# A transformer kernel's first mixers: weighted sums written already turned, and the order of work around the last gate products

## The reference, cut to what matters

```python
gates = sigmoid(gate_logits)                    # 3 per nsa head
# nsa: 8 heads, three branches on the same queries
o_c = softmax(q @ k_compressed) @ v_compressed  # 15 compressed keys
o_s = softmax(q @ k_slc) @ v_slc                # 8 passes, "slc"
o_w = softmax(q @ k_win) @ v_win                # 8 passes, "win"
y_a = g0 * o_c + g1 * o_s + g2 * o_w
# moba: 8 heads of their own keys, causal       # 8 passes, "moba"
y_b = softmax(q @ k) @ v
gate_a, gate_b = split(sigmoid(h @ w_gbr))
merged = gate_a * (y_a @ w_up_nsa) + gate_b * (y_b @ w_up_moba)
x = x + g_m * (merged @ w_out)
```

## Time and profile before

| | |
|---|---|
| median of 3 runs | 2048.45 us |
| the profiled execution's own time | 2048.88 us |
| its span (first to last instruction) | 2047.0 us |
| PE busy | 1998.6 us, 98% |
| DVE busy | 1465.8 us, 72% |
| ACT busy | 1093.2 us, 53% |
| DMA, mean | 182 GB/s |

### The profile page before, as it was taken

How to read it: one execution, slowest core, us unless ns; L and a number is a source line. 1 busy time by engine, 2 the same in 40 slices (tenths; PEclk the granted TensorE clock), 3 DMA queues, 4 the chain that set the end, 5 groups by cost and what they waited for, 6 DMA issues and landing times. The chain is left out here.

```text
span 2047.0 us, 32169 instructions
## 1 busy us (share of the span) xinstructions
PE 1998.6 (98%) x12934; PEld 1775.0 (87%) x12934; DVE 1465.8 (72%) x2326; ACT 1093.2 (53%) x1732; POOL 23.6 (1%) x46
## 2 busy tenths in 40 slices
PE   7999999999999999999999999999999999999999
PEld 4889898898788988898888779888898899899888
DVE  7887778867786686567766676677667757767774
ACT  3555545535656455545545656655455536855552
POOL 1001000000010000000000000000000000000000
PEclk9999999999999999999999999999999999999999
DMA  9455458856455466555556324355555554235554
GB/s 353 157 205 196 167 181 275 273 207 187 145 201 211 147 224 206 185 186 185 186 190 201 125 102 144 130 187 187 186 177 187 186 181 137 93 124 163 187 175 134
DMA packets 266212, 372.23 MB, mean 182 GB/s; under 512 B 8400, under 2 KB 160336, under 8 KB 266064
## 3 DMA queue, kind: packets, MB, share of 16 engines
q1 hardware_dynamic: 264736, 368.91, 54.2%
q10 hardware_dynamic: 1328, 1.26, 0.2%
HBM read 369.09 MB, written 1.05 MB: 181 GB/s over the span
## 5 line engine op out<-in xcount | busy, mean ns | idle before, releaser
L2302 DVE TENSOR_TENSOR parts<-ring,parts 128x2048 fp32r<-128x2048 f32 (+2 forms) x304 | 675.8, 2223 | 396.1 <-ACT parts L721 395.4
L721 ACT ACTIVATE parts<-ring 128x2048 fp32r<-128x2048 f32 (+2 forms) x304 | 565.5, 1860 | 560.9 <-PE psum L1513 317.0
L1513 PE MATMUL psum<-h,parts 128*128 128x512 f32 x1920 | 675.9, 397 | 0.0
L1511 PE MATMUL psum<-h,parts 128*128 128x256 f32 x1920 | 539.0, 281 | 0.7 <-DVE parts L2302 0.5
L1513 PEld LDWEIGHTS psum<-h,parts 128*128 128x128 f32 x1920 | 360.6, 188 | 87.0
L1511 PEld LDWEIGHTS psum<-h,parts 128*128 128x128 f32 x1920 | 362.3, 189 | 2.5 <-DVE parts L2302 2.3
L1505 PE MATMUL psum<-h,parts 128*128 128x256 f32 (+1 forms) x2088 | 265.0, 285 | 4.5 <-DVE h L2311 2.0
L1505 PEld LDWEIGHTS psum<-h,parts 128*128 128x128 f32 (+1 forms) x2088 | 253.9, 190 | 7.3 <-issue 5.0
L1505 PE MATMUL psum<-parts,h 128*128 128x512 f32 (+1 forms) x864 | 204.9, 388 | 5.2 <-DVE h L2311 2.9
L1505 PE MATMUL psum<-hid_hl,parts 128*128 128x256 f32 x1584 | 189.4, 281 | 0.8 <-DVE parts L2302 0.6
L1505 PEld LDWEIGHTS psum<-hid_hl,parts 128*128 128x128 f32 x1584 | 188.0, 188 | 2.4 <-DVE parts L2302 2.4
(11 more groups left out here) (265 smaller groups left out, 2116.7 us busy)
## 6 DMA issues: line engine op xcount, KB each, us to landing
ring<-in_w_ffn_in SPq DMA_DIRECT2D x88, 512.0 KB, 4.8
ring<-in_ffn_w_gate SPq DMA_DIRECT2D x88, 512.0 KB, 3.7
ring<-in_ffn_w_up SPq DMA_DIRECT2D x88, 512.0 KB, 4.7
ring<-in_w_ada SPq DMA_DIRECT2D x43, 1024.0 KB, 5.4
ring<-in_w_in SPq DMA_DIRECT2D x36, 1024.0 KB, 5.0
ring<-in_ffn_w_down SPq DMA_DIRECT2D x32, 1024.0 KB, 4.9
ring<-in_w_ffn_out SPq DMA_DIRECT2D x16, 1024.0 KB, 5.1
ring<-in_ffn_w_down SPq DMA_DIRECT2D x16, 768.0 KB, 4.5
```

The costliest lines, as they stand in the source:

```text
L721: act.activation(out, in_, func, **kw).then_inc(*sig(name, *keys))
L1511: pe.matmul(bank[:, 0:S], wt_hl[1], act[:, 0, :], start=start, stop=False, skip_group_check=True)
L1513: return pe.matmul(bank.rearrange("p (a s) -> p a s", a=2), wt_hl[0], act, start=False, stop=stop, skip_group_check=True)
L2302: dve.tensor_tensor(out, a, b, op).then_inc(*sig(name, *keys))
```

## The change

Values become stationary: a pair of heads (n and n+1) writes its weighted sums by feature into partitions 0 to 63 and 64 to 127 of one bank (`turned_place`), with 256 moving columns for the first 128 keys and 128 for the second. slc, win and the compressed branch add up in banks 4 and 5, moba in 6 and 7. As the sums come out by feature, gate over sum must be applied earlier, by token: DVE makes `factor` for each head, and ACT multiplies the probabilities by it (`scaled`) ahead of the turning. The turning is three rounds behind the scores (`LATER`), and the loop has 28 rounds. The probabilities have four buffers and the turned ones three, instead of three and two. The transposes of `y`, `branch`, `moba_out` and the copy of the compressed output go; the compressed product is done at round 11, as four products of 256 columns. Gate products 6 and 7 are copied out ahead of any sigmoid. On DVE the splits at the last step of `gbr` go, so that the splits beyond w_up_nsa 0 come behind the products with the gates.

```diff
-HEADS, LAG, UNITS = 24, 2, 2
+HEADS, LAG, LATER, UNITS = 24, 2, 3, 2
...
+        def turned_place(bank, n):
+            half, c = HD * (n % 2), S * (n // 2 % 2)
+            return psum[half:half + HD, bank + n // 4, c:c + S]
...
@@ ACT
+            def scaled(head, n):
+                st, i = head["st"], head["i"]
+                buf = shifted_of(st, n)
+                act.wait_ge(*at(("factor", st, i)))
+                for t, (a, b) in enumerate(spans(head["mask"])):
+                    run(buf[:, a:b], buf[:, a:b], ACT.Copy, "act_scaled", ("scaled", st, i, t),
+                        scale=factor[:, n % 4, t:t + 1])
...
                             if n == 1 and k == 3 and i == 3:
-                                act.wait_ge(*at(("copied", ("gbr", l, 5))))
-                                run(br_gates[:, 1, 0:4], br_gates[:, 1, 0:4], ACT.Sigmoid,
-                                    "act_step")
                                 for q in (6, 7):
-                                    ...
-                                run(br_gates[:, 0], br_gates[:, 0], ACT.Sigmoid, "act_gates",
-                                    ("gates", l, 0))
+                                    copies(("gbr", l, q), br_e[:, 2 * q:2 * q + 2, :])
+                                act.wait_ge(*at(("copied", ("gbr", l, 7))))
+                                for a in range(2):
+                                    run(br_gates[:, a], br_gates[:, a], ACT.Sigmoid, "act_gates",
+                                        ("gates", l, a))
                                 act.preload_act_table_set(EXP_LN)
...
-                    if LAG <= i < HEADS + LAG:
-                        m = i - LAG
+                    if LATER <= i < HEADS + LATER:
+                        m = i - LATER
                         turned_copy(heads[m], base + m)
...
+                    if 1 <= i <= HEADS:
+                        scaled(heads[i - 1], base + i - 1)
...
@@ PE
+                def weighted_pair(i, first, done):
+                    pair = heads[i:i + 2]
+                    pe.wait_ge(*at(("copied", ("turn", pair[1]["st"], pair[1]["i"]))))
+                    probs = [prob_of(head["st"], base + i + n) for n, head in enumerate(pair)]
+                    for t, (a, c, q0) in enumerate(((0, S, 0), (S, S + P, P))):
+                        for n, head in enumerate(pair):
+                            ...
+                            mm = pe.matmul(head["o"][:, q0:S], head["v"][t], moving,
+                                           start=first and t == 0, stop=t == 1,
+                                           skip_group_check=True)
...
-            def moba_turn(l, j):
-                ...
-                for i in range(HEADS + LAG + 1):
+                for i in range(HEADS + LATER + 1):
                     if i < HEADS:
                         scores(i)
-                    if LAG <= i < HEADS + LAG:
-                        turn(i - LAG)
+                    if LATER <= i < HEADS + LATER:
+                        turn(i - LATER)
                     if i == 23:
                         next(more, None)
-                    if i > LAG:
-                        weighted(i - LAG - 1)
+                    if i > LATER and (i - LATER - 1) % 2:
+                        weighted_two(i - LATER - 2)
...
-                    if i == 6:
-                        ... (two products of 512 columns)
+                    if i == 11:
+                        compressed_out()
...
-                    if i == 21: ... tr y
-                    if i == 24:
-                        moba_turn(l, 0)
...
@@ DVE
-                                if k == 3:
+                                if k == 3 and (i, n) != (3, 1):
                                     splits.until((("gbr", l), i, n), 2)
...
-                def moba_out(p, pv): ...
-                def branch(b, kind): ...
+                def scaled(i):
+                    ...
+                    dve.wait_ge(*at(("probs", st_, head["i"], 1)))
+                    total, out = sums[:, column, :], factor[:, (base + i) % 4, :]
+                    ...
+                    if st_[0] == "moba":
+                        dve.reciprocal(out, total).then_inc(*sig("dve_step", done))
+                    else:
+                        dve.reciprocal(out, total).then_inc(*sig("dve_step"))
+                        settle()
+                        tt(out, out, gate[:, :, head["n"], 1 if st_[0] == "slc" else 2],
+                           ALU.mult, "dve_step", done)
...
                     if i < HEADS:
                         masked(heads[i]["st"], heads[i]["i"], con("causal"), HD ** -0.5)
+                    if 1 <= i <= HEADS:
+                        scaled(i - 1)
...
-                    if i == 7: ... (copies of the compressed output)
-                    if i == 11:
-                        branch(1, "slc")
-                    if i == 19:
-                        branch(2, "win")
```

More of the change, by code:

```diff
@@ L526, in paired @@
                          v=[v[:, t, HD * n:HD * n + HD] for t in range(TT)],
[L527 to L528 removed]
+                         o=turned_place(6, n)) for n in range(8)]
         def diff_heads():
@@ L1064, in first_block @@
                             copies(("tr mk", l, j), mk_t[:, 2 * j:2 * j + 2, :])
[L1065 to L1068, removed]
+                    if i in (16, 20):
+                        j = i // 20
+                        y_copies(("tr y", l, 0, j), 2 * j, y_mix)
+                    if i == 24:
                         y_copies(("tr y", l, 1, 0), 4, y_mix)
@@ L1730, in weighted @@
                         [("attended", head["st"])] if head["last"] else [])))
-                return scores, turn, weighted
+                def weighted_pair(i, first, done):
[4 more added lines that the diff above has]
+                        for n, head in enumerate(pair):
+                            if t == 0:
+                                moving = probs[n][:, 0:S]
+                            else:
+                                moving = probs[n][:, S:S + P]
+                            mm = pe.matmul(head["o"][:, q0:S], head["v"][t], moving,
+                                           start=first and t == 0, stop=t == 1,
+                                           skip_group_check=True)
+                    mm.then_inc(*sig("pe_out", ("pv", base + i), ("pv", base + i + 1), *done))
+                return scores, turn, (weighted_pair if tiled(heads[0]["st"]) else weighted)
             pe.wait_ge(*at("loaded const"))
@@ L1881, in first_block, with weighted_two, compressed_out @@
                                      8: [("copied", ("tr kw", l))],
[L1882 to L1885, removed]
+                                     16: [("copied", ("tr mq", l, 1)), ("copied", ("tr mk", l, 1))]})
+                def weighted_two(m):
+                    if m % 8 == 0:
+                        pe.wait_ge(*at(("tok", (("win", l, (1, 2, 5)[m // 8]), 1))))
+                    mixer, j = m // 16, m % 8 // 4
+                    job = ("tr y", l, mixer, j)
+                    first = m % 4 == 0 and m // 8 != 1
+                    if first:
+                        open_bank(job, (4 + 2 * mixer + j,))
+                    weighted(m, first, [("full", job)] if m % 4 == 2 and m >= 8 else [])
+                def compressed_out():
+                    pe.wait_ge(*at(("copied", ("cmp turn", l))))
+                    pe.wait_ge(*at(("v diag", l)))
+                    for c in range(4):
+                        pe.matmul(psum[:, 4 + c // 2, S * (c % 2):S * (c % 2) + S],
+                                  v_diag[:, P * c:P * c + P],
+                                  cmp_pt.rearrange("p t q -> p (t q)"), start=False, stop=True,
+                                  skip_group_check=True)
                 def compressed_scores(t):
@@ L1945, in first_block @@
                                         for a in range(2) for t in range(TT)],
[L1946 to L1952, removed]
-                    if i == 24:
-                        moba_turn(l, 0)
+                                       [("head", l, "mk", t) for t in range(TT)], SIDE)
                     if i in ADA_AT and pending:
-                        ada_cols(*pending.pop(0), SIDE if i < 10 else (4, 5))
+                        ada_cols(*pending.pop(0), SIDE if i < 20 else (4, 5))
                 whole_of(more)
-                moba_turn(l, 1)
                 for g in range(2):
@@ L2762, in beside @@
                             yield
[L2764 to L2789, removed]
-                        bank = 4 + 2 * (b - 1) + t
-                        out = rot[:, t, :].rearrange("p (h d) -> p h d", d=HD)
-                        acc = psum[:, bank, :].rearrange("p (h d) -> p h d", d=HD)
-                        tt(out, acc, over(wt[:, t, 0:8], 8, HD), ALU.mult, "dve_freed",
-                           ("free", ("out", (kind, l), bank)))
+                def scaled(i):
```

(12 more changed lines are left out.)

98 lines of the change are left out of this document (41 added, 57 removed).

## The result

The changed kernel takes 2065.3 us (median of 5 runs, 2061.38 to 2069.26) against 2047.73 before in the same runs. The ratio is 1.0085, 95% interval 1.007 to 1.010: slower, by 17.6 us. The profiled execution took 2065.79 us, with a span of 2064.0 and a mean granted clock of 0.992 (before 0.998).

A forecast was written before the change was run, and what follows sets the result against it. PE's own work was taken as the bound. Per layer -1.8 -1.5 -1.8 +1.05 +6.2 +1.2 = +3.35, for two layers +6.7 on 2048.45, giving 2055 us; own range 2050 to 2060, full range 2044 to 2066.

The forecast's parts named there:

- rival 1: Weighted sums of head pairs: the halves don't overlap at all, a pair takes 1.63 us, total 2066; chance 16%.
- third wait: Behind the last gate products, before the second w_up_nsa part: PE waits 5.8 us for DVE's low part, before 0.8.
- rival 3: Behind the gates: the low part is made before PE comes, so that 5.8 us wait is absent; 2041, chance 12%.
- rival 4: Behind the gates: ada's half panel is added earlier, only the low part is late; 2049, chance 10%.
- second wait: Behind the last gate products, ahead of a pair: PE waits 2.8 us for a turned copy behind ACT's tables and sigmoids.
- first wait: Right behind the last gate products: PE waits 0.4 us for ACT's copies instead of 1.98, winning 1.6.
- clock: Behind the gates: PE's long waits bring a half-clock dip, +1.2 us per layer, between 0 and 1.7.
- pairs: Mixer loop: two heads' weighted sums cost 1.19 us together instead of 1.34; 12 pairs win 1.8 us per layer.
- rival 2: Weighted sums of head pairs: full overlap and free form, 0.65 us, 2042; milder, 0.98 us, 2050; chance 12% for both.
- start of the loop: First rounds: ACT's factor copies delay compressed keys, +0.65, and DVE is behind around round 6, +0.4; together +1.05 us per layer.
- transposes: Mixer loop: 16 transposes of y leave PE at 0.11 us each, saving 1.8 us per layer.
- -1.5: Mixer loop: waits for the compressed product (0.9) and at the opening of moba's bank (0.6) go, per layer.

The follow-up runs named there:

- experiment 1: Changed kernel with DVE's splits at the last step of gbr put back: 2052.32 us, ratio 1.0020.
- experiment 3: Kernel before the change, with only DVE's splits at the last step of gbr removed: 2064.9 us, ratio 1.0082.
- Experiment 4: Changed kernel with ACT's two sigmoids and table loads moved from gbr's last step into the next step: 2056.03 us, ratio 1.0035.
- experiment 6: The version of experiment 5 with ACT's factor copies moved to the end of each round, except the last head's: 2039.51 us, ratio 0.9955.
- experiment 5: Changed kernel with DVE's splits at gbr's last step back and ACT's sigmoids and table loads one step later: 2038.22 us, ratio 0.9950.
- experiment 2: Changed kernel with 20 and 48 idle bf16 products filling PE's two long waits behind the gate products: 2055.8 us, ratio 1.0044.
- experiment 7: The version of experiment 5 with each pair issued head by head instead of in turn: 2039.33 us, ratio 0.9954.
- experiment 8: The version of experiment 5 with factor copies of heads 0, 1 and 14 moved behind copies PE waits for: 2038.98 us, ratio 0.9957.

## Why the prediction was right, and where its sizes were off

The forecast was slower by 6.7 us, 2055; measured was 2065.3, slower by 17.6. The sign and the mechanism held; the sum missed 11 us. That the number still lies in the stated range, 2044 to 2066, is luck: it is outside the forecast's own 2050 to 2060, and the range reached to 2066 only for rival 1, halves that never overlap, which the trace shows to be false.

**The third wait, the step that decides: right.** 5.8 was forecast, 5.96 is there. The order on DVE is the forecast one, and experiments 1 and 3 show it from both sides. Rivals 3 and 4 fall.

**The second wait: right.** 2.8 was forecast, 2.65 is there. Experiment 4 takes it away by the cause given for it, ACT's block of tables and sigmoids.

**The first wait: too small.** 0.4 was forecast, 0.94 is there. The forecast took one of the two copies as made before PE's step ends; ACT starts both behind it (211.26 for 210.99), since it has the factor copies of head 22 (0.79) to do first. In experiment 6, which puts those behind, the wait is 0.4.

**The clock: the mis-sized term.** It stood in the sum with 1.2 us a layer, 1.7 at most, for one dip. Each layer has 10.2 us at half clock behind the gates, since each of the two long waits brings its own stretch. In the first layer this costs 0.68 on the pair, 0.9 on the 24 products behind it and 2.35 on the 24 at 231.02, together 3.9; in the second, read the same way, 3.7. The bound of 1.7 came from the one stretch of 3.4 in the earlier trace rows; 6.8 us in one piece had no row before. The second layer has 6.8 more in its first rounds, which the prediction did not have at all and whose cause is open: the wait just ahead of it, 1.6 us for the compressed keys, is the same in the first layer and in both layers of experiment 5, and there no stretch at half clock follows. Its cost is some 2.3 us net (below). Together that is 9.9 us where the sum had 2.4, and experiment 2, in whose profile all five stretches are gone, puts them at 9.5. That is 7 of the 11 us missing.

**The pairs: right in kind, too small in size.** The halves overlap fully and the form costs what the scores' form costs: rival 2 in its milder form (0.98 a pair). The round with a pair takes 5.20 us (186.92 to 192.12) and the one without 4.20, so a pair costs 1.00: the 0.65 of one head's records and 0.35 for the form. A pair of rounds is 0.34 shorter, not 0.15, so 12 pairs win 4.1 a layer instead of 1.8. The failing assumption was that starts keep the order of issue; experiment 7 shows that a half does not wait for the other half's earlier record. The Trainium skill's rule that tiles run in parallel ("TensorEngine Tiling (Array Packing)", Key Properties) agrees with the trace: eight records go through in 0.80 us that one after the other would take 1.30. The Trainium skill's rule in the same section, that a change of tiling mode drains the engine, agrees with the 0.35 us that a pair costs above its records.

**The start of the loop: too small.** +1.05 was forecast, and the rows show +1.0 (compressed keys, 1.6 for 0.6), +0.9 (FILL bank) and +1.2 (moba's keys), 3.1. The cause given (ACT's factor copies stand ahead of other copies) holds for the compressed keys and moba's keys, by experiment 8, but was charged for the first alone. It does not hold for the FILL bank, by experiments 6 and 8: there ACT is itself held up by DVE, and PE comes 0.6 earlier than before (109.03 for 109.61), as these rounds have no weighted sums yet.

**What cancels.** Without the clock the first layer's sum is -1.8 (transposes, not measured apart) -1.5 -4.1 + 3.1 + 6.75 (9.55 for 2.8) = +2.4; with 3.9 for the clock +6.3. Loop start to the first product of w_out took 245.34 - 88.38 = 157.0 before and 252.25 - 88.20 = 164.0 after, +7.1, so 0.8 is unexplained. In the second layer the same distance grew by 9.2; from the 2.1 more, and the 0.2 less behind its gates, comes the 2.3 for its first rounds. Of the 17.0 by which the span grew, 0.7 is outside the loops. There 516.4 to 519.8 before has no stretch to answer it after, and the one near 1223 is 6.8 long instead of 3.4; the two nearly cancel. In the prediction's own terms, for two layers, the pairs were 4.6 us too dear, the start 4.1 and the waits behind the gates 1.1 too cheap. Together they leave only 0.6, and that is luck as well.

## What to carry to other kernels

Moving an operation ahead of another on a strict queue moves the other one behind everything the first waits for. Before such a move, walk the list of what is behind it (here a low part that PE needs at once, with a half panel in front) and give each its new earliest time. And where the bound engine waits for several microseconds, count the clock beside the wait: here the waits behind the gates grew by 6.75 us a layer, and half clock took 3.7 to 3.9 more from the work behind them.

## What the runs showed of the hardware

- Two products whose outputs lie in different halves of the partitions (128x64 stationaries, fp32, 256 moving columns) start 6 ns apart, and their first records are both through in 0.44 us, where the first is 0.43 long. From the first of a pair's eight records to the next product it is 0.80 us, and 0.81 when they are issued head by head; with what it adds in front, a pair costs its round 1.00 us.
- A wait of PE of 2.65 us was followed by a stretch of 3.4 us at half clock (1.2 GHz), one of 5.96 by 6.8 us, of which 1.4 fell into the wait itself. After a wait of 1.96 us there were 3.4 us at half clock in experiment 3, and none after one of 1.98 before. Where a wait as long as the one of 5.96 us was filled with 48 idle bf16 products, the clock stayed at 1.00.
- Twenty-four fp32r products of 256 columns took 5.26 us at half clock and 2.91 at full.
